# Gate stage of a two-block expert kernel: one-hot rows of the first index made on GpSimd

## Chip, cores and metric

The kernel runs on one core of one Trainium2 chip. The metric is device time in microseconds of one execution, the median over several runs. Lower is better.

## What is computed

Two transformer blocks run one after the other on 256 tokens of width 1024, all in float32. Each block ends in a layer of product-key experts. The part of it that matters here, cut from the reference:

```python
qh = (t @ w_q).reshape(T, PEER_HEADS, 2, PEER_KEY_DIM // 2)
s = jnp.einsum('thpd,hpnd->thpn', qh, sub_keys)           # 128 keys per half
s_top, i_top = lax.top_k(s, PEER_TOPK)                    # 16 of each half
best, pos = lax.top_k(cand.reshape(T, PEER_HEADS, 256), PEER_TOPK)
idx = ...                                                 # i1 * 128 + i2
g = jax.nn.softmax(best, axis=-1)
act = jax.nn.gelu(jnp.einsum('thkd,td->thk', u_tab[idx], t))
out = jnp.einsum('thk,thkd->td', g * act, v_tab[idx])
```

Each token chooses 8 heads x 16 = 128 experts of 128 x 128 = 16384, each named by a first index, a second index and a gate.

## The kernel before, in words

The kernel gathers no expert rows. For each block it streams both whole tables (128 units of 512 KB each) and multiplies densely. In the **u loop** TensorE makes, for every unit, the products of 128 experts with all 256 tokens, and ScalarE writes their GELU into `arena` (`acts`, 128 experts x 128 units x 256 tokens). In the **v loop** the same array, multiplied by the gates, is contracted with the v table. Both loops split float32 into a rounded part and a rest: ScalarE casts (L1377, L1599), VectorE subtracts (L1380, L1606), TensorE does three passes (L1308 to L1310).

Between the two loops stands the **gate stage**, once per block. It turns the chosen pairs of indices into a dense table of gates and multiplies `acts` by it. It takes the 256 tokens in 32 groups of 8 (`NG = 32`). For a group:

- VectorE copies the group's five columns per token out of `sel` into `stage[slot]` (L1535, 128x40): first index, second index, gate, minus the second index, minus the gate; the partition is the choice. It raises the semaphore `staged`.
- VectorE makes `hot1` in one instruction (L1537, 128x1024): for each of the 8 tokens, row k of a 128x128 tile is 1 at the first index of choice k and 0 elsewhere.
- `hot2`, the same with the second index and the gate in place of 1, is shared. VectorE makes tokens 4 to 7 with one two-operation instruction each (L1540, 128x128, equality with the second index, then times the gate). ScalarE makes tokens 0 to 3 in two instructions each (L1549: absolute distance to the index; L1553: Relu of gate minus gate times distance). `ACT_HOT = 4` is this number.
- TensorE (`pe_gates`, L1565) multiplies hot1 by hot2 for each of the 8 tokens into two of the eight PSUM banks.
- VectorE (`dve_multiply`, L1574, 128x1024) multiplies the group's 8 token columns of `acts` by those two banks, in place.

Order and waits. hot1, hot2 and `stage` have four slots, and so has PSUM (two banks each). VectorE's order is written out by hand: hots of group 0, hots of 1, then for each g: hots of g + 2, multiply of g (`HOT_AHEAD = 2`). Before it stages a group, VectorE waits until TensorE has used the slot's former group (`e_ready`). TensorE waits for both makers of the hots (`hots_dve`, `hots_act`) and for the multiply four groups back (`gated`). The multiply waits for `e_ready` of its own group. When all 32 are multiplied, ScalarE, VectorE and TensorE enter the v loop together. The stream's ring (four units) is filled by the SP queue, which stands still during this stage since nothing consumes. GpSimd runs one instruction of the program, a memset of a 128x128 tile of ones at its very start (L1753), and nothing after it.

All hots read `iota`, a 128x128 constant loaded at the start (`common_loaded`).

Of the kernel before, what the change touches and what calls it, by code (L numbers as in the profile page):

```python
# [26 lines left out]
ALU = mybir.AluOpType  # L27
# [3 lines left out]
P = 128  # L31
# [20 lines left out]
HLRING = 4  # L52
CRING = 4
GRING = 4
ACT_HOT = 4
NPROJ = 3
B_STAT = (3, 7)
B_SCORE = (4, 5)
# [191 lines left out]
def build(nc, stream, xT, ctxT, metaT, vectors, common, consts1, consts2, keys1, keys2, w_a2, out):  # L250
# [45 lines left out]
    def c_(name):  # L296
        a, n = con_at[name]
        return con[:, a:a + n]

    ident, blk64, iota, ones = c_("ident"), c_("blk64"), c_("iota"), onesbuf[:, :]  # L300
# [23 lines left out]
    def S(name):  # L324
        if name not in sems:
            sems[name] = nc.alloc_semaphore(name)
        return sems[name]
# [114 lines left out]
    hot1 = gbuf[:, 0:GRING * 8 * P].rearrange("p (r t i) -> p r t i", r=GRING, t=8)  # L442
    hot2 = gbuf[:, GRING * 8 * P:2 * GRING * 8 * P].rearrange("p (r t i) -> p r t i", r=GRING, t=8)
    H = Space(gbuf, 10240)
    H.take(8192)
    stage = [H.take(KINDS, 8) for _ in range(GRING)]
    hot_dist = [H.take(ACT_HOT, P) for _ in range(2)]

# [450 lines left out]
    class Rope:  # L899
# [14 lines left out]
        def pe(self, eng):  # L914
            for r in self.ready:
                wait(eng, *r)
            for i, (src, _) in enumerate(self.items):
                m = self.r0 + i
                wait(eng, "rope_read", m - 1)
                eng.matmul(ps[:, B_STAT[m % 2], 0:self.n], self.rot, src, start=True, stop=True).then_inc(S("rope_swapped"), 1)  # L920
# [482 lines left out]
    def topk_part(eng, i, s, half):  # L1403
# [16 lines left out]
        if n == 3:  # L1420
            for x, _, rest in halves_of:
                eng.max(topbuf[:, x, 8:16], rest)
# [102 lines left out]
    NG = T // 8  # L1525
    HOT_AHEAD = 2

    def base(b):

        return (b - 1) * (NG + GRING)  # L1530

    def dve_hots(dve, b, g, slot_):

        dve.wait_ge(S("e_ready"), g + (base(b) + 1))
        dve.tensor_copy(stage[slot_], sel[:, :, ds(g * 8, 8)]).then_inc(S("staged"), 1)  # L1535
        dve.wait_ge(S("staged"), g + ((b - 1) * NG + 1))
        dve.tensor_tensor(hot1[:, slot_, :, :], stage[slot_][:, 0, :].rearrange("p (t o) -> p t o", o=1).broadcast_to([P, 8, P]),  # L1537
                          iota.rearrange("p (o i) -> p o i", o=1).broadcast_to([P, 8, P]), ALU.is_equal)
        for t in range(ACT_HOT, 8):
            ins = dve.tensor_scalar(hot2[:, slot_, t, :], iota, stage[slot_][:, 1, t:t + 1],  # L1540
                                    stage[slot_][:, 2, t:t + 1], ALU.is_equal, ALU.mult)
        ins.then_inc(S("hots_dve"), 1)

    def act_hots(act, b, g, slot_):

        act.wait_ge(S("staged"), g + ((b - 1) * NG + 1))
        st, dist = stage[slot_], hot_dist[slot_ % 2]
        for t in range(ACT_HOT):
            ins = act.activation(dist[:, t, :], iota, ACT.Abs, bias=st[:, 3, t:t + 1])  # L1549
        ins.then_inc(S("hot_dist_ready"), 1)  # L1550
        act.wait_ge(S("hot_dist_ready"), g + ((b - 1) * NG + 1))
        for t in range(ACT_HOT):
            ins = act.activation(hot2[:, slot_, t, :], dist[:, t, :], ACT.Relu, bias=st[:, 2, t:t + 1], scale=st[:, 4, t:t + 1])  # L1553
        ins.then_inc(S("hots_act"), 1)

    def e_banks(slot_):
        return ps[:, 2 * slot_:2 * slot_ + 2, :].rearrange("p s n -> p (s n)")

    def pe_gates(pe, b, g, slot_):

        pe.wait_ge(S("hots_dve"), g + ((b - 1) * NG + 1))
        pe.wait_ge(S("hots_act"), g + ((b - 1) * NG + 1))
        pe.wait_ge(S("gated"), g + (base(b) + 1))
        for t in range(8):
            mm = pe.matmul(e_banks(slot_)[:, t * P:(t + 1) * P], hot1[:, slot_, t, :], hot2[:, slot_, t, :],  # L1565
                           start=True, stop=True)
        mm.then_inc(S("e_ready"), 1)
# [8 lines left out]
    def ds(a, n):  # L1576
        return bass.ds(a, n) if not isinstance(a, int) else slice(a, a + n)
# [44 lines left out]
    def peer_pe(pe, b):  # L1622

        pe.wait_ge(S("peer_in"), b)
        pe.drain().then_inc(S("split_used"), HLRING)
        pe.wait_ge(S("hsplit_ready"), b)
        u_loop("pe", pe, b, 0, NQ // UB, table="wq")
        peer_pe_scores(pe, b)
        pe.wait_ge(S("peer_s_copied"), 8 * b)
        with pe.Fori(0, TOPK_IT) as i:  # L1630
            for s in range(TOPK_UB):
                u_unit("pe", pe, b, i, s, TOPK_UB)
        for n in range(MID_UNITS):
            u_unit("pe", pe, b, 0, MID_AT + n)
            pe_gate_part(pe, b, n)
        u_loop("pe", pe, b, MID_END // UB, N_IT)

        pe.wait_ge(S("u_bank_free"), banks_freed(b + 1, "wq"))
        pe.wait_ge(S("sel_taken"), b)
        pe.drain().then_inc(S("e_ready"), GRING)  # L1640
        pe.drain().then_inc(S("gated"), GRING)
        with pe.Fori(0, NG // GRING) as i:
            for n in range(GRING):
                pe_gates(pe, b, i * GRING + n, n)
        pe.wait_ge(S("gated"), b * (NG + GRING))
        v_loop("pe", pe, b)
# [29 lines left out]
    def peer_dve(dve, b):  # L1676
# [11 lines left out]
        for g in range(HOT_AHEAD):  # L1688
            dve_hots(dve, b, g, g)
        with dve.Fori(0, NG // GRING - 1) as i:  # L1690
            for n in range(GRING):
                dve_hots(dve, b, i * GRING + (n + HOT_AHEAD), (n + HOT_AHEAD) % GRING)
                dve_multiply(dve, b, i * GRING + n, n)
        for g in range(NG - GRING, NG):
            if g + HOT_AHEAD < NG:
                dve_hots(dve, b, g + HOT_AHEAD, (g + HOT_AHEAD) % GRING)
            dve_multiply(dve, b, g, g % GRING)
# [13 lines left out]
    with nc.Block() as block:  # L1711
        @block.sync
        def _(sp):

            peer_units = {u: n for n, u in enumerate(m for key in ("wq1", "u1", "v1", "wq2", "u2", "v2") for m in units[key])}

            def load(u):
                sp.dma_start(slot(u), stream[u, :, :]).then_inc(S(arrival(u)[0]), 16)

            u = 0  # L1720
            while u < n_units:
                old = u - RING
                if u in peer_units and old in peer_units:

                    end = u
                    while end < n_units and end in peer_units:
                        end += 1
                    rounds = (end - u) // RING
                    n0 = peer_units[old]
                    with sp.Fori(0, rounds) as i:  # L1730
                        for s in range(RING):
                            sp.wait_ge(S("split_lo"), i * 2 * RING + 2 * (n0 + s + 1))
                            sp.dma_start(slot(u + s), stream[bass.ds(i * RING + (u + s), 1), :, :]
                                         .rearrange("a p n -> (a p) n")).then_inc(S(ring_full[(u + s) % RING]), 16)
                    u += rounds * RING
                    while u < end:
                        sp.wait_ge(S("split_lo"), 2 * (peer_units[u - RING] + 1))
                        load(u)
                        u += 1
                    continue  # L1740
                if old in peer_units:
                    sp.wait_ge(S("split_lo"), 2 * (peer_units[old] + 1))
                elif old >= 0:
                    sp.wait_ge(S("tile_done"), last_tile[old] + 1)
                load(u)
                u += 1
            sp.wait_ge(S("peer_out"), 2 * KD)
            sp.dma_start(out, resid[:, :, :]).then_inc(S("out_stored"), 16)
            sp.wait_ge(S("out_stored"), 16)

        @block.gpsimd
        def _(pool):
            pool.memset(ones, 1.0).then_inc(S("ones_ready"), 1)  # L1753

        @block.scalar
        def _(act):
# [167 lines left out]
```

## Time and profile before

| | before |
|---|---|
| runs | 2661.96, 2658.42, 2659.87 us; median 2659.87 |
| profiled execution, span from first to last instruction | 2658.5 us |
| TensorE busy | 2445.7 us (92%) |
| VectorE busy | 1683.0 us (63%) |
| ScalarE busy | 1293.7 us (49%) |
| GpSimd busy | 0.4 us |
| mean granted TensorE clock | 0.973 of 2.4 GHz |

The profiled execution has no time of its own beside its span. The span lies 1.4 us below the median of the runs and 0.1 us above the fastest of them. How to read the profile: a group of instructions is one line of the code on one engine with its shapes, its count, its total busy time and the mean duration of one instruction. Instructions on one engine overlap a little, so the step from start to start is shorter than a duration. Idle time before an instruction is put down to the instruction that ended it.

### The profile page before, as it was taken

Reading aid. Unit: us, or ns where it says so; the run is one execution under the profiler, and the core shown is the slowest. Engines: PE = TensorE matmul, PEld = TensorE weight load, DVE = VectorE, ACT = ScalarE, POOL = GpSimd, SP = SyncE. Lnnn points to the kernel's source line nnn. Section 1 sums busy time; section 2 is a strip of 40 time slices with the busy share of each in tenths; the row PEclk is TensorE's granted clock in tenths of the full one; section 3 lists DMA queues with packets and bytes.
Section 4 is the critical chain, followed back from the end, with each engine's and each line's share of the span. In section 5 each row is a group of like instructions: output and inputs, shape, how many; then the busy total and the mean of one; then the engine's idle time right before and its main releaser. Section 6 shows DMA issues by size and latency. Waiting matters only on the chain.

```text
span 2658.5 us, 51578 instructions
## 1 busy us (share of the span) xinstructions
PE 2445.7 (92%) x17556; PEld 2270.0 (85%) x17556; DVE 1683.0 (63%) x3490; ACT 1293.7 (49%) x2816; POOL 0.4 (0%) x5
## 2 busy tenths in 40 slices
PE   7999979999985799999799999889999985899998
PEld 2767879999985799999677777789999985899998
DVE  2565247888769766665225674238888769766665
ACT  1456145555568655554123422055555568555554
POOL 0000000000000000000000000000000000000000
PEclk9989989999999999999899899999999999999999
DMA  6345444555530355555232212445555530355554
GB/s 229 136 168 189 150 143 163 183 183 181 184 119 0 103 182 182 183 183 178 98 127 88 80 56 80 135 142 183 181 181 182 183 103 0 121 182 183 183 184 143
DMA packets 108502, 388.94 MB, mean 146 GB/s; under 512 B 12784, under 2 KB 15088, under 8 KB 107776
## 3 DMA queue, kind: packets, MB, share of 16 engines
q1 hardware_dynamic: 104256, 380.16, 42.5%
q10 hardware_dynamic: 4160, 7.61, 0.9%
q8 instruction: 58, 0.95, 0.1%
q14 instruction: 28, 0.23, 0.0%
HBM read 386.67 MB, written 1.05 MB: 146 GB/s over the span
## 4 chain that ended last, share of the span: by engine, by line
PE 84%; DVE 9%; issue 3%; ACT 2%; DVEq 0%; ACTq 0%; DMA 0%; PEld 0%; PEldq 0%
PE ps L1308 20%; PE ps L1310 20%; PE ps L1309 20%; PE ps L707 19%; DVE arena L1574 2%; DVE gbuf L1540 2%; PE ps L789 2%; PE ps L1000 1%; PE ps L978 1%; PE ps L1565 1%; PE ps L1340 1%; DVE gbuf L801 0%; PE ps L992 0%; PE ps L1236 0%; ACT arena L772 0%
## 5 line engine op out<-in xcount | busy, mean ns | idle before, releaser
L1308 PE MATMUL ps<-hsplit,hl 128*128 128x256 f32 x2304 | 655.9, 285 | 31.7 <-DVE hl L1380 31.7
L1309 PE MATMUL ps<-hsplit,hl 128*128 128x256 f32 x2304 | 655.0, 284 | 0.0
L1310 PE MATMUL ps<-hsplit,hl 128*128 128x256 f32 x2304 | 654.9, 284 | 0.0
L1308 PE MATMUL ps<-csplit,hl 128*128 128x256 f32 x2048 | 581.1, 284 | 6.2 <-DVE hl L1606 6.2
L1309 PE MATMUL ps<-csplit,hl 128*128 128x256 f32 x2048 | 581.0, 284 | 0.0
L1310 PE MATMUL ps<-csplit,hl 128*128 128x256 f32 x2048 | 581.0, 284 | 0.0
L1377 ACT CAST hl<-ring 128x512 fp32r<-128x512 f32 x576 | 355.6, 620 | 387.2 <-PE ps L1310 386.8
L1380 DVE TENSOR_TENSOR hl<-ring,hl 128x512 fp32r<-128x512 f32 x576 | 397.6, 692 | 221.2 <-ACT hl L1377 187.4
L1308 PEld LDWEIGHTS ps<-hsplit,hl 128*128 128x128 f32 x2304 | 445.7, 193 | 32.8 <-ACT hl L1377 32.8
L707 PE MATMUL ps<-arena,ring 128*128 128x256 f32 (+2 forms) x1896 | 447.6, 395 | 15.5 <-issue 10.8
L1309 PEld LDWEIGHTS ps<-hsplit,hl 128*128 128x128 f32 x2304 | 445.7, 193 | 0.0
L1310 PEld LDWEIGHTS ps<-hsplit,hl 128*128 128x128 f32 x2304 | 445.4, 193 | 0.0
L707 PEld LDWEIGHTS ps<-arena,ring 128*128 128x128 f32 x1896 | 369.2, 197 | 78.8 <-issue 25.7
L1606 DVE TENSOR_TENSOR hl<-ring,hl 128x512 fp32r<-128x512 f32 x512 | 354.3, 693 | 92.8 <-ACT hl L1599 91.6
L1308 PEld LDWEIGHTS ps<-csplit,hl 128*128 128x128 f32 x2048 | 394.6, 193 | 6.5 <-issue 6.5
L1310 PEld LDWEIGHTS ps<-csplit,hl 128*128 128x128 f32 x2048 | 394.6, 193 | 0.0
L1309 PEld LDWEIGHTS ps<-csplit,hl 128*128 128x128 f32 x2048 | 394.6, 193 | 0.0
L1599 ACT CAST hl<-ring 128x512 fp32r<-128x512 f32 x512 | 315.8, 617 | 109.9 <-PE ps L1310 109.9
L1603 DVE TENSOR_TENSOR csplit<-arena,csplit 128x256 fp32r<-128x256 f32 x256 | 109.0, 426 | 183.0 <-ACT csplit L1598 183.0
L1598 ACT CAST csplit<-arena 128x256 fp32r (+1 forms) x256 | 104.2, 407 | 235.5 <-PE ps L1310 228.5
L1565 PE MATMUL ps<-gbuf 128*128 128x128 f32 x1024 | 133.0, 285 | 92.7 <-ACT gbuf L1553 49.1
L1565 PEld LDWEIGHTS ps<-gbuf 128*128 128x128 f32 x1024 | 122.2, 196 | 103.4 <-issue 52.2
(196 smaller groups left out, 2019.7 us busy)
## 6 DMA issues: line engine op xcount, KB each, us to landing
ring<-stream SPq DMA_DIRECT2D x723, 512.0 KB, 3.3
arena<-keys ACTq DMA_DIRECT2D x2, 1024.0 KB, 4.9
gbuf<-consts ACTq DMA_DIRECT2D x1, 1120.0 KB, 5.1
arena<-xT ACTq DMA_DIRECT2D x1, 1024.0 KB, 10.4
arena<-ctxT ACTq DMA_DIRECT2D x1, 1024.0 KB, 12.7
resid<-xT ACTq DMA_DIRECT2D x1, 1024.0 KB, 8.9
out<-resid SPq DMA_DIRECT2D x1, 1024.0 KB, 3.9
gbuf<-consts ACTq DMA_DIRECT2D x1, 832.0 KB, 6.3
```

Source lines behind the costliest of these rows:

```text
L707: mm = pe.matmul(ps[0:t.rows, t.bank, 0:t.cols], lhs, rhs, start=(t.start and i == 0), stop=(t.stop and i == last))
L789: mm = eng.matmul(ps[:, bank, 0:self.cols], self.lhs, self.squares[:, k, 0:self.cols], start=(i == 0), stop=(i == len(group) - 1))
L1308: pe.matmul(out_ap, w[0], m[0], start=start, stop=False)
L1309: pe.matmul(out_ap, w[1], m[0], start=False, stop=False)
L1310: return pe.matmul(out_ap, w[0], m[1], start=False, stop=stop)
L1377: eng.copy(hl[:, hslot, 0, :], raw).then_inc(S("split_hi"), 1)
L1380: eng.tensor_tensor(hl[:, hslot, 1, :], raw, hl[:, hslot, 0, :].bitcast(F32), ALU.subtract)\
L1565: mm = pe.matmul(e_banks(slot_)[:, t * P:(t + 1) * P], hot1[:, slot_, t, :], hot2[:, slot_, t, :], start=True, stop=True)
L1598: eng.copy(csplit[:, cslot, 0, :], acts[:, c]).then_inc(S("csplit_hi"), 1)
L1599: eng.copy(hl[:, hslot, 0, :], slot(unit)[:, part]).then_inc(S("split_hi"), 1)
L1603: eng.tensor_tensor(csplit[:, cslot, 1, :], acts[:, c], csplit[:, cslot, 0, :].bitcast(F32), ALU.subtract)
L1606: eng.tensor_tensor(hl[:, hslot, 1, :], slot(unit)[:, part], hl[:, hslot, 0, :].bitcast(F32), ALU.subtract).then_inc(S("split_lo"), 1)
```

## The change

GpSimd gets a loop over both blocks and all 32 groups. For each group it waits for `staged` and makes hot1 in eight instructions of 128x128, one per token, and token 3 of hot2. ScalarE makes tokens 0 to 2. VectorE no longer makes hot1, and still makes tokens 4 to 7 of hot2. TensorE waits for a third semaphore, `hots_pool`.

```diff
-ACT_HOT = 4
+ACT_HOT = 3
+POOL_HOT = 1
 ...
         dve.tensor_copy(stage[slot_], sel[:, :, ds(g * 8, 8)]).then_inc(S("staged"), 1)
         dve.wait_ge(S("staged"), g + ((b - 1) * NG + 1))
-        dve.tensor_tensor(hot1[:, slot_, :, :], stage[slot_][:, 0, :].rearrange("p (t o) -> p t o", o=1).broadcast_to([P, 8, P]),
-                          iota.rearrange("p (o i) -> p o i", o=1).broadcast_to([P, 8, P]), ALU.is_equal)
-        for t in range(ACT_HOT, 8):
+        for t in range(ACT_HOT + POOL_HOT, 8):
             ins = dve.tensor_scalar(hot2[:, slot_, t, :], iota, stage[slot_][:, 1, t:t + 1],
                                     stage[slot_][:, 2, t:t + 1], ALU.is_equal, ALU.mult)
         ins.then_inc(S("hots_dve"), 1)
+
+    def pool_hots(pool, b, g, slot_):
+
+        pool.wait_ge(S("staged"), g + ((b - 1) * NG + 1))
+        st = stage[slot_]
+        for t in range(8):
+            pool.tensor_scalar(hot1[:, slot_, t, :], iota, st[:, 0, t:t + 1], None, ALU.is_equal)
+        for t in range(ACT_HOT, ACT_HOT + POOL_HOT):
+            ins = pool.tensor_scalar(hot2[:, slot_, t, :], iota, st[:, 1, t:t + 1], st[:, 2, t:t + 1],
+                                     ALU.is_equal, ALU.mult)
+        ins.then_inc(S("hots_pool"), 1)
 ...
         pe.wait_ge(S("hots_act"), g + ((b - 1) * NG + 1))
+        pe.wait_ge(S("hots_pool"), g + ((b - 1) * NG + 1))
 ...
             pool.memset(ones, 1.0).then_inc(S("ones_ready"), 1)
+            pool.wait_ge(S("common_loaded"), 16)
+            for b in (1, 2):
+                for g in range(NG):
+                    pool_hots(pool, b, g, g % GRING)
```

## Rows read from the trace of the kernel before

**Rows 1.** Timeline of the first gate stage, its start: start us, us, engine, line, work

```profile
776.43 0.19 DVE L1535 COPY gbuf<-s_area 128x40 f32<-128x40 f32 x1 [4.94 <-PEq L1640]
776.66 1.22 DVE L1537 TENSOR_TENSOR gbuf<-gbuf,con 128x1024 f32<-128x1024 f32 x1
779.72 5.44 PE L1565 MATMUL ps<-gbuf 128*128 128x128 f32 x32 [3.85 <-ACT gbuf L1553]
783.60 1.21 DVE L1574 TENSOR_TENSOR arena<-arena,ps 128x1024 f32 x1
```

**Rows 2.** Timeline of the first gate stage, its end and the v loop's first instruction

```profile
885.68 2.34 DVE L1574 TENSOR_TENSOR arena<-arena,ps 128x1024 f32<-128x1024 f32 x2
886.58 2.02 PE L1565 MATMUL ps<-gbuf 128*128 128x128 f32 x16 [1.51 <-DVE gbuf L1540]
888.64 1.22 DVE L1574 TENSOR_TENSOR arena<-arena,ps 128x1024 f32<-128x1024 f32 x1 [0.61 <-PE ps L1565]
889.89 0.40 ACT L1598 CAST csplit<-arena 128x256 fp32r<-128x256 f32 x1 [3.41 <-DVE arena L1574]
```

**Rows 3.** Timeline of the second gate stage: its first instruction and the one behind it

```profile
2165.66 0.19 DVE L1535 COPY gbuf<-s_area 128x40 f32<-128x40 f32 x1 [4.94 <-PEq L1640]
...
2279.29 0.40 ACT L1598 CAST csplit<-arena 128x256 fp32r<-128x256 f32 x1 [3.57 <-DVE arena L1574]
```

**Rows 4.** Timeline in the middle of the first gate stage: one whole group

```profile
841.05 0.19 DVE L1535 COPY gbuf<-s_area 128x40 f32 x1
841.27 1.23 DVE L1537 TENSOR_TENSOR gbuf<-gbuf,con 128x1024 f32<-128x1024 f32 x1
841.27 1.28 ACT L1549 ACTIVATE gbuf<-con,gbuf 128x128 f32<-128x128 f32 x4 [0.56 <-DVE gbuf L1535]
842.42 1.11 DVE L1540 TENSOR_SCALAR gbuf<-con,gbuf 128x128 f32<-128x128 f32 x4
842.59 1.65 ACT L1553 ACTIVATE gbuf<-gbuf 128x128 f32<-128x128 f32 x4
843.44 1.21 DVE L1574 TENSOR_TENSOR arena<-arena,ps 128x1024 f32 x1
844.33 2.02 PE L1565 MATMUL ps<-gbuf 128*128 128x128 f32 x16 [1.50 <-DVE gbuf L1540]
844.57 0.18 DVE L1535 COPY gbuf<-s_area 128x40 f32 x1
```

**Rows 5.** Groups by line and shape, 782 to 884 us: busy us, mean ns | idle before

```profile
L1553 ACT ACTIVATE gbuf<-gbuf 128x128 f32<-128x128 f32 x118 | 48.6, 482 | 1.0
L1549 ACT ACTIVATE gbuf<-con,gbuf 128x128 f32<-128x128 f32 x118 | 37.8, 390 | 15.4 <-DVE gbuf L1535 15.4
L1540 DVE TENSOR_SCALAR gbuf<-con,gbuf 128x128 f32<-128x128 f32 x116 | 32.2, 341 | 0.0
```

**Rows 6.** Busy time in 5 us stretches: PE, PEld, DVE, ACT, POOL, PEclk, DMA, GB/s

```profile
775.00:780.00 5.00, 1.15 (x10) 0.98 (x9) 3.50 (x8) 3.69 (x11) 0.00 (x0) 1.00 0.00 2
780.00:785.00 5.00, 5.00 (x32) 4.96 (x30) 4.93 (x14) 4.93 (x15) 0.00 (x0) 0.66 0.00 0
840.00:845.00 5.00, 2.69 (x22) 2.56 (x23) 4.93 (x11) 3.85 (x11) 0.00 (x0) 1.00 0.00 0
```

**Rows 7.** Timeline of GpSimd, the whole span

```profile
0.24 0.10 POOL L1918 MEMSET const-float32-0.0<- 128x1 f32 x1 [0.24 <-issue]
0.74 0.20 POOL L1753 MEMSET onesbuf<- 128x128 f32 x1 [0.29 <-POOLq L1918]
```

**Rows 8.** Groups by line and shape on VectorE, the whole span

```profile
L801 DVE RECIPROCAL gbuf<-gbuf 128x256 f32<-128x256 f32 x20 | 35.1, 1753 | 0.7
L1185 DVE TENSOR_TENSOR arena<-gbuf 128x128 f32<-128x128 f32 x56 | 12.5, 285 | 0.3
...
L1506 DVE TENSOR_SCALAR s_area<-ps 128x256 f32<-128x256 f32 x2 | 0.8, 419 | 0.0
L1469 DVE TENSOR_SCALAR gbuf<-gbuf 128x256 f32<-128x256 f32 x2 | 0.6, 285 | 0.0
```

## The prediction

> **What bounds the kernel now.** I read the page first: TensorE carries the span, and only the two gate stages lie between its long loops. So I read each gate stage by its edges, then one group in its middle, then its groups of instructions. In the timeline the first stage begins with the copy at 776.43 us and ends with the last multiply, 888.64 + 1.22 = 889.86 us; the first cast of the v loop starts 0.03 us later [rows 1, 2]. The second stage runs from 2165.66 to just before 2279.29 us [rows 3]. That is 113.4 and 113.6 us, 227 us together, 8.5% of the span. All that follows waits for it, so a microsecond here is a microsecond of the kernel.
>
> Within a stage one group takes 844.57 - 841.05 = 3.52 us, and VectorE is never idle in it [rows 4]: in the stretch from 840 to 845 us it is busy 4.93 of 5 us, TensorE 2.69, ScalarE 3.85 [rows 6]. By start-to-start steps, VectorE's group is the copy with its own wait 0.22 us, hot1 1.15, four rows of hot2 1.02, the multiply 1.13. ScalarE has slack: 1.32 us to the start of the Relus and 1.65 for them, 2.97 in all, and it sits idle 0.56 us for the copy. TensorE needs 2.02 us and waits 1.50 [rows 4]. From the last group's matmuls to the end there are 2.06 us of TensorE and 1.22 of multiply [rows 2]. VectorE is the bound, and no DMA moves: the DMA share is 0.00 [rows 6].
>
> **The change part by part.**
>
> *hot1 leaves VectorE.* One instruction per group, 1.15 us by the step. VectorE is left with 0.22 + 1.02 + 1.13 = 2.37 us per group. That is the floor on this engine.
>
> *One row of hot2 leaves ScalarE.* Two instructions per group. An Abs steps by (1.28 - 0.39) / 3 = 0.30 us and a Relu by (1.65 - 0.48) / 3 = 0.39 us [rows 4, 5], so ScalarE goes from 2.97 to about 2.3 us. It was not the bound. It matters only where the others fall near 2.4 us, where four rows would have held the group at 2.97.
>
> *TensorE's third wait.* It is one more instruction in TensorE's queue ahead of matmuls that wait 1.50 us anyway; I cost it at nothing. What is queued behind it are the group's matmuls and then, in VectorE's queue, the multiply and the staging of the third group on. The stage has room for that. From the end of GpSimd's group g to its group g + 3 being staged are about 2.06 + 1.22 + 0.2 = 3.5 us, against two groups of GpSimd's work in between.
>
> *GpSimd's nine instructions.* This is the new term, and everything turns on it. They stand in one queue with nothing else in it; the wait for `common_loaded` was over hundreds of microseconds before. If one takes t, GpSimd needs 9t per group, from the first staging at 776.66 us on [rows 1]. If it sets the pace, the stage ends at 776.66 + 32 x 9t + 3.4, the last being TensorE's 2.06, the multiply's 1.22 and about 0.1 of hand-over. Setting that equal to 889.86 gives 9t = 3.43 us, t = 0.381 us: **the break-even**. Each 0.01 us on t moves the kernel by 64 x 9 x 0.01 = 5.8 us.
>
> The trace of before has no GpSimd instruction that reads. The nearest from below is the memset of 128x128, 0.20 us; the memset of 128x1 takes 0.10, so a fixed part of 0.10 and another 0.10 for 128 columns that are only written [rows 7]. The upper end, far off, is VectorE's slow reciprocal, 1.753 us for 256 columns, so some 0.9 for 128, the price of an operation that takes many steps per element [rows 8]. Ends: 9t = 1.8 and 8.1 us. Between them I build from the nearest row. To the memset's 0.20 I add 0.10 for 128 columns read, 0.10 for 128 comparisons (one more turn of the same loop each), and 0.06 for fetching the per-partition operand: VectorE's instruction with such operands takes 0.341 us where one of the same size without takes 0.285 [rows 5, 8]. That is t = 0.46 us. I take it for the two-operation row too. ScalarE's instructions of this shape, 0.39 and 0.48 us, lie on both sides of it [rows 5]. So 9t = 4.14 us against 3.52 today. The stage ends at 776.66 + 132.5 + 3.4 = 912.5 us, 22.7 us later; two stages make **+45 us**. VectorE falls idle 4.14 - 2.37 = 1.8 us per group, and TensorE waits for GpSimd.
>
> The Trainium skill, "GPSIMD Engine Reference", section 3.1, gives a best case of 1.8 cycles per element at 1.2 GHz for a tight loop, with further fixed costs (section 7: about 102 cycles for a read command). An estimate from that page is 0.19 + 0.09 = 0.28 us for one instruction, by which the change would gain; the trace of before shows no such instruction.
>
> *TensorE's clock.* It is granted 1.00 in the middle of the stage, with TensorE idle 1.50 us out of 3.52, and 0.66 in the stretch behind the 3.85 us of idleness at its start [rows 4, 6]. At 4.14 us per group the idle stretch is 2.1 us. If the grant fell to 1.2 GHz, the matmuls would take 4.04 us, still under 4.14, so only the last group would show it, 2 us per stage. I cost it at nothing.
>
> The sum is made on the profiled execution, 2658.5 + 45.4 = 2703.9 us. The median of the runs lies 1.4 us above that span, so **2705 us**, 1.7% slower. A measurement of this kernel can tell about 0.2%, 5.3 us, from no change.
>
> **The rivals.**
>
> *GpSimd is fast enough (the other side).* Place: the same nine instructions. Below t = 0.381 us the change gains, until at t = 0.26 us VectorE's 2.37 us take over. At t = 0.30 us GpSimd still sets the pace: 776.66 + 86.4 + 3.4 = 866.5, 23.4 us earlier per stage, 2613 us. With VectorE the bound, 32 x 2.37 = 75.8 us and some 2.7 for the first products give a stage of 78.5, 35 us less, 2590 us. For it speak the memset's 0.10 us for 128 columns, and the slack on ScalarE and TensorE, which can both follow to 2.4. Against it, a memset reads nothing and compares nothing. I give the paced gain 0.24 and the VectorE floor 0.14.
>
> *GpSimd and VectorE take turns.* Both now work at the same time on the same memory. If a VectorE instruction that reads and writes only that memory with one input shuts GpSimd out, and the reverse, the copy (0.19) and the four rows of hot2 (1.11) add to GpSimd's time: 4.14 + 1.30 = 5.44 us per group. The stage ends at 776.66 + 174.1 + 3.4 = 954.2, 64.3 us later, and the kernel takes 2789 us. The durations of L1540 on VectorE would then scatter upward from 0.341. For it: with its source in SBUF a 128x256 instruction takes 0.285 us, with its source in PSUM 0.419, so the former moves the columns at about twice the rate, as if by a second path [rows 8]. Against it: no trace of before has the two engines at work together. Chance 0.15. With this in force, break-even is at t of about 0.24 us, so it would also eat a fast GpSimd's gain. The rule is one of the Trainium skill, "SBUF — State Buffer", section "Who interferes with whom": a VectorE instruction in a 2-port mode and a GpSimd instruction hold the shared port pair in turn, each for its whole length. The two durations agree with its 2-port mode; no run here shows the lock.
>
> *GpSimd is slower still.* At t above 0.6 us, the lines above give more than 2786 us, up to 2959 at 0.9. Chance 0.05.
>
> *Nothing visible.* 9t near 3.43 us, within 0.08 either way: 0.06.
>
> **How the numbers follow.** The forecast's case, GpSimd alone setting the pace with t between 0.39 and 0.6 us, has 0.36. Slower: 0.36 + 0.15 + 0.05 = 0.56. Faster: 0.24 + 0.14 = 0.38. Same: 0.06. The likeliest case's own range is 2665 to 2786 us. The range that should hold the time 8 times in 10 must take in both signs: it goes down to the VectorE floor, 2588, and up to the taking of turns, 2792. Outside lie the very slow GpSimd and about half of the taking of turns, where t is above 0.46 too, and a small rest below.
>
> **What would show it.** In the profile after, GpSimd has 576 new instructions of 128x128, and their step from start to start is t. Right: the period of L1535 is 9t, over 3.52 us, TensorE's idle time before L1565 is put down to GpSimd, VectorE waits before L1574, ScalarE waits longer before L1549, and the u and v loops are unchanged. The prediction is wrong if a step is under 0.38 us, or if VectorE's L1540 grows and its group no longer fits in 2.37 us, or if time appears outside the two stages.

## The result and the profile after

The changed kernel takes 2790.51 us (median), against 2659.55 us for the kernel before in the runs beside it: ratio 1.0491, interval 1.0478 to 1.0504. It is 131 us slower where the prediction had 45 slower. The profiled execution spans 2789.3 us.

The page of the kernel after: busy time by engine, GpSimd and the clock in 40 slices, and the chain that ended last.

```profile
PE 2511.3 (90%) x17556; PEld 2333.3 (84%) x17556; DVE 1625.0 (58%) x3426; ACT 1249.7 (45%) x2688; POOL 350.5 (13%) x581
POOL 0000000000089600000000000000000099400000
PEclk9989999999977799999899899999999977799999
PE 79%; POOL 13%; DVE 4%; ACT 2%; issue 1%; DMA 0%; ACTq 0%; PEld 0%; DVEq 0%; POOLq 0%; PEldq 0%
L1548 POOL TENSOR_SCALAR gbuf<-con,gbuf 128x128 f32<-128x128 f32 x512 | 300.5, 603 | 2052.7 <-DVE gbuf L1536 2052.7
```

GpSimd is busy only in the two gate stages, and there without a gap. It holds 13% of the chain; before, the larger part of the chain in these stages was VectorE's hot2 rows and multiplies (L1540 and L1574, 2% of the whole span each). The lines have moved: L1548 is the hot1 rows on GpSimd, L1550 its hot2 row, L1539 VectorE's rows (L1540 before), L1576 the products (L1565), L1585 the multiply (L1574).

Timeline of the kernel after, one stretch of the first stage (start, length, work; in brackets the idle time and what ended it), answering to [rows 4]:

```profile
844.29 0.18 DVE L1536 COPY gbuf<-s_area 128x40 f32 x1
844.51 1.24 DVE L1539 TENSOR_SCALAR gbuf<-con,gbuf 128x128 f32<-128x128 f32 x4
845.41 0.84 POOL L1550 TENSOR_SCALAR gbuf<-con,gbuf 128x128 f32<-128x128 f32 x1
846.24 4.64 POOL L1548 TENSOR_SCALAR gbuf<-con,gbuf 128x128 f32<-128x128 f32 x8
846.55 3.60 PE L1576 MATMUL ps<-gbuf 128*128 128x128 f32 x16 [3.54 <-POOL gbuf L1550]
850.30 1.22 DVE L1585 TENSOR_TENSOR arena<-arena,ps 128x1024 f32 x1 [4.55 <-PE ps L1576]
850.87 0.79 POOL L1550 TENSOR_SCALAR gbuf<-con,gbuf 128x128 f32<-128x128 f32 x1
851.63 4.85 POOL L1548 TENSOR_SCALAR gbuf<-con,gbuf 128x128 f32<-128x128 f32 x8
```

Everyone waits for GpSimd: TensorE 3.54 us, and VectorE for TensorE 4.55 us. GpSimd's own steps from start to start are 4.63 / 8 = 0.58 us for a row of hot1 and 0.76 and 0.83 for the row of hot2, some 0.78. Two starts 28 groups apart, and the end of the stage, from the same execution:

```profile
791.50 4.64 POOL L1548 TENSOR_SCALAR gbuf<-con,gbuf 128x128 f32<-128x128 f32 x8
...
944.83 4.63 POOL L1548 TENSOR_SCALAR gbuf<-con,gbuf 128x128 f32<-128x128 f32 x8
...
952.56 1.22 DVE L1585 TENSOR_TENSOR arena<-arena,ps 128x1024 f32<-128x1024 f32 x1 [2.41 <-PE ps L1576]
953.81 0.40 ACT L1609 CAST csplit<-arena 128x256 fp32r<-128x256 f32 x1 [13.19 <-DVE arena L1585]
```

A group takes (944.83 - 791.50) / 28 = 5.48 us, where it took 3.52. The stage starts at 774.54 and ends at 953.8: 179.3 us against 113.4 [rows 1, 2]. That is 65.9 us more. The second stage takes 180.4 us against 113.6, 66.8 us more. Together they make some 133 us, where the two profiled spans differ by 130.8: all of the loss lies in the two stages.

### The profile page after: what moved, and what is told of

Read it like the earlier page. It is cut to its first block, busy times and chain, and to the rows that moved or that the text cites. A ratio compares the mean times of both kernels' runs of the same rounds, so it can differ in the third digit from the quotient of the medians.

```text
span 2789.3 us, 51997 instructions
## 1 busy us (share of the span) xinstructions
PE 2511.3 (90%) x17556; PEld 2333.3 (84%) x17556; DVE 1625.0 (58%) x3426; ACT 1249.7 (45%) x2688; POOL 350.5 (13%) x581
## 4 chain that ended last, share of the span: by engine, by line
PE 79%; POOL 13%; DVE 4%; ACT 2%; issue 1%; DMA 0%; ACTq 0%; PEld 0%; DVEq 0%; POOLq 0%; PEldq 0%
PE ps L1309 19%; PE ps L1310 19%; PE ps L1311 19%; PE ps L708 18%; POOL gbuf L1548 11%; POOL gbuf L1550 2%; PE ps L790 1%; PE ps L1001 1%; PE ps L979 1%; PE ps L1341 1%; DVE gbuf L802 0%; DMA ring<-stream 0%; PE ps L993 0%; PE ps L1237 0%; ACT arena L773 0%
## 5 line engine op out<-in xcount | busy, mean ns | idle before, releaser
L1548 POOL TENSOR_SCALAR gbuf<-con,gbuf 128x128 f32<-128x128 f32 x512 | 300.5, 603 | 2052.7 <-DVE gbuf L1536 2052.7
L1576 PE MATMUL ps<-gbuf 128*128 128x128 f32 x1024 | 200.8, 376 | 157.4 <-POOL gbuf L1550 145.5
L1576 PEld LDWEIGHTS ps<-gbuf 128*128 128x128 f32 x1024 | 186.0, 281 | 172.1 <-issue 91.3
```

Of the source, the lines that this page charges most:

```text
L1548: pool.tensor_scalar(hot1[:, slot_, t, :], iota, st[:, 0, t:t + 1], None, ALU.is_equal)
```

## The experiments

Two theories stood after the result. Theory A: GpSimd's own price is higher than the 0.46 us that I built up. Theory B: the price was about right, and the rest comes from GpSimd and VectorE taking turns, the second rival, whose 2789 us is almost exactly the measured time. The number alone can't tell them apart.

**e1, hot1 alone on GpSimd.** One execution.

```diff
-ACT_HOT = 3
-POOL_HOT = 1
+ACT_HOT = 4
+POOL_HOT = 0
```

> GpSimd makes hot1 alone (8 instructions per group), ScalarE again makes four rows of hot2. Theory A, GpSimd's own price sets the pace (0.585 us per hot1 row, 0.78 for the hot2 row, by the steps in the trace after): a group takes 8 x 0.585 = 4.7 us in place of 5.5, and each stage ends 25 us earlier than after the change, some 2740 us in all. Theory B, the time comes mostly from GpSimd and VectorE taking turns: VectorE's instructions are the same, so a group still carries their 1.3 us, and a group takes 8 x 0.46 + 1.3 = 5.0 us.

It took 2743.5 us. The first stage ran from 779.3 to 932.9 us, 153.6 us, and GpSimd's groups start 4.67 us apart. That is theory A's number, where theory B had 5.0.

**e2, no rows by VectorE.** One execution.

```diff
+        dve.wait_ge(S("e_ready"), base(b) + GRING)
+        dve.memset(hot2[:, :, 4:8, :], 0.0).then_inc(S("hots_dve"), 1)
...
-        for t in range(ACT_HOT + POOL_HOT, 8):
-            ins = dve.tensor_scalar(...)
-        ins.then_inc(S("hots_dve"), 1)
...
-        pe.wait_ge(S("hots_dve"), g + ((b - 1) * NG + 1))
+        pe.wait_ge(S("hots_dve"), b)
```

> VectorE makes no rows of hot2 in the loop (rows 4 to 7 are zeros, so the gates of those tokens are left out): only the copy and the multiply stand beside GpSimd. Theory A (own price): GpSimd's steps stay at about 0.58 us, a group takes 5.4 us, the time falls by under 8 us against the changed kernel. Theory B (turns with VectorE's single-input instructions): GpSimd's steps fall to about 0.46 us and a group to 4.3 us, some 2715 us in all.

It took 2793.2 us. GpSimd's timeline in it:

```profile
940.45 4.69 POOL L1544 TENSOR_SCALAR gbuf<-con,gbuf 128x128 f32<-128x128 f32 x8
945.08 0.84 POOL L1546 TENSOR_SCALAR gbuf<-con,gbuf 128x128 f32<-128x128 f32 x1
945.85 4.69 POOL L1544 TENSOR_SCALAR gbuf<-con,gbuf 128x128 f32<-128x128 f32 x8
```

With VectorE's four rows gone, a group still takes 945.85 - 940.45 = 5.40 us. The turns were worth 5.48 - 5.40 = 0.08 us per group to GpSimd, not 1.30: for this change theory B falls. The stages are a little shorter, 177.9 us against 179.3 and 178.3 against 180.4, 3.5 us together. The whole time did not drop, since the rest of this execution was 5.6 us longer (it entered the first stage at 778.2 us and not at 774.5). The four runs of the changed kernel differ by more than that, from 2788 to 2796 us.

**e3, a price list.** The kernel before with nine GpSimd instructions per group beside it, writing to free memory. They stand here in the order of the lines below. TensorE still waits for the semaphore that the last of the nine raises, so the list sets the pace of the stage. One execution.

```diff
+        pool.memset(z[0], 0.0)
+        pool.tensor_copy(z[1], iota)
+        pool.tensor_scalar(z[2], iota, 3.0, None, ALU.is_equal)
+        pool.tensor_scalar(z[3], iota, st[:, 0, 0:1], None, ALU.is_equal)
+        pool.tensor_scalar(z[4][:, 0:64], iota[:, 0:64], st[:, 0, 0:1], None, ALU.is_equal)
+        pool.tensor_scalar(s_area[:, 1024:1280], con[:, 0:256], st[:, 0, 0:1], None, ALU.is_equal)
+        pool.tensor_scalar(z[5], iota, st[:, 0, 0:1], None, ALU.mult)
+        pool.tensor_tensor(z[6], iota, ident, ALU.subtract)
+        pool.tensor_scalar(z[7], iota, st[:, 1, 0:1], st[:, 2, 0:1], ALU.is_equal, ALU.mult)
```

> The kernel before, with nine GpSimd instructions per group beside it whose results are not used: memset, copy, compare with a constant, compare with a per-partition operand at 128, 64 and 256 columns, multiply, subtract of two tensors, compare and multiply. The prediction's working: 0.20 us for the memset, 0.30 for the copy, 0.40 for the comparison with a constant, 0.46 with a per-partition operand. Rival: the fixed part is what was missed, so 64 columns cost nearly as much as 128 (0.45 or more against 0.58), and 256 columns 0.8. Other rival: the work per column was missed, so 64 columns cost about 0.3 and 256 about 1.1 us.

It took 2793.7 us, with a new group every 5.54 us. Timeline of GpSimd over one group; VectorE is idle beside it from the memset to the subtraction:

```profile
853.51 0.20 POOL L1553 MEMSET s_area<- 128x128 f32 x1
853.66 0.29 POOL L1554 COPY s_area<-con 128x128 f32<-128x128 f32 x1
853.92 0.54 POOL L1555 TENSOR_SCALAR s_area<-con 128x128 f32<-128x128 f32 x1
854.44 0.60 POOL L1556 TENSOR_SCALAR s_area<-con,gbuf 128x128 f32<-128x128 f32 x1
855.02 0.44 POOL L1557 TENSOR_SCALAR s_area<-con,gbuf 128x64 f32<-128x64 f32 x1
855.43 0.92 POOL L1558 TENSOR_SCALAR s_area<-con,gbuf 128x256 f32<-128x256 f32 x1
856.32 0.61 POOL L1559 TENSOR_SCALAR s_area<-con,gbuf 128x128 f32<-128x128 f32 x1
856.90 0.45 POOL L1560 TENSOR_TENSOR s_area<-con 128x128 f32<-128x128 f32 x1
857.34 0.80 POOL L1561 TENSOR_SCALAR s_area<-con,gbuf 128x128 f32<-128x128 f32 x1
```

From start to start: memset 0.15 us, copy 0.26, comparison with a constant 0.52, with a per-partition operand 0.58, the same at 64 columns 0.41 and at 256 columns 0.89, multiplication 0.58, subtraction of two tensors 0.44; compare and multiply lasts 0.80. The step from copy to arithmetic with one operand, 0.26 us, is as large as the copy. It isn't the comparison, since a multiplication costs the same. From the three widths a column costs 2.4 to 2.7 ns, which leaves a fixed part of 0.58 - 128 x 0.0025 = 0.26 us. The measured 0.41 and 0.89 us lie between the two rivals of the expectation, nearer to the one with the fixed part.

The same view a group earlier, with VectorE's hot1 (L1538, two inputs in SBUF) beside GpSimd:

```profile
847.26 1.25 DVE L1538 TENSOR_TENSOR gbuf<-gbuf,con 128x1024 f32<-128x1024 f32 x1
847.41 1.51 POOL L1555 TENSOR_SCALAR s_area<-con 128x128 f32<-128x128 f32 x1
...
850.87 1.36 DVE L1538 TENSOR_TENSOR gbuf<-gbuf,con 128x1024 f32<-128x1024 f32 x1
851.36 1.18 POOL L1560 TENSOR_TENSOR s_area<-con 128x128 f32<-128x128 f32 x1
```

An instruction of 0.54 us takes 1.51, one of 0.45 takes 1.18; both end 0.3 to 0.4 us behind the end of L1538. So turns do exist, against the two-input instruction that the change had taken off VectorE. Another group shows both sides, a memset and a copy that start while L1538 runs:

```profile
863.64 1.22 DVE L1538 TENSOR_TENSOR gbuf<-gbuf,con 128x1024 f32<-128x1024 f32 x1
863.85 0.20 POOL L1553 MEMSET s_area<- 128x128 f32 x1
864.00 1.01 POOL L1554 COPY s_area<-con 128x128 f32<-128x128 f32 x1
```

The copy takes 1.01 us instead of 0.29. The memset (L1553) lasts between 204 and 205 ns in all its 64 places, and 28 of them lie inside L1538. The Trainium skill, "SBUF — State Buffer", section "Who interferes with whom", says that a VectorE instruction with two SBUF inputs contends with a GpSimd instruction that reads SBUF, and not with one that only writes it. This trace agrees: the reads are held up, the memset is not.

**e4, three rows of hot2 on GpSimd, hot1 back on VectorE.** Rows of hot2: ScalarE 3, GpSimd 3, VectorE 2.

```diff
-POOL_HOT = 1
+POOL_HOT = 3
+        dve.tensor_tensor(hot1[:, slot_, :, :], ...)
-        for t in range(8):
-            pool.tensor_scalar(hot1[:, slot_, t, :], ...)
```

> hot1 is back on VectorE; GpSimd makes three rows of hot2 (tokens 3 to 5), ScalarE three, VectorE two. Theory A (own price): GpSimd 3 x 0.78 = 2.35 us per group, VectorE 0.22 + 1.15 + 0.51 + 1.13 = 3.0 us, ScalarE 2.3: VectorE sets the pace at 3.0 to 3.1 us against 3.52 before, 26 to 33 us faster than before, about 2630 us. Theory B (turns): the 1.15 us of hot1 and the others on VectorE add to GpSimd's 2.35, so 3.5 us or more, no gain over before.

2640.96 us, ratio to before 0.9922 (0.9905 to 0.9938): faster than before. Two steps in its timeline, and the group of GpSimd's rows from 790 to 880 us:

```profile
841.25 1.25 DVE L1538 TENSOR_TENSOR gbuf<-gbuf,con 128x1024 f32<-128x1024 f32 x1
844.29 1.25 DVE L1538 TENSOR_TENSOR gbuf<-gbuf,con 128x1024 f32<-128x1024 f32 x1
```
```profile
L1550 POOL TENSOR_SCALAR gbuf<-con,gbuf 128x128 f32<-128x128 f32 x87 | 88.3, 1028 | 0.9 <-DVE gbuf L1536 0.9
```

The group takes 3.04 us as theory A had it, with VectorE full. But GpSimd is full too: a row lasts 1.03 us on average instead of 0.79. Of the 31 us only 20 came, since the stage is 103.4 us, 6.4 more than 32 groups of 3.03, while before it was 0.8 more than 32 groups of 3.52 [rows 1, 2, 4]: the ends of the stage give back a part.

**e5, the same without hot1.** hot1 is zero, set once per stage by VectorE.

```diff
-        dve.tensor_tensor(hot1[:, slot_, :, :], ...)
+        dve.wait_ge(S("e_ready"), base(b) + GRING)
+        dve.memset(hot1, 0.0)
```

> The last kernel (three rows of the second index on GpSimd), but VectorE makes no rows of the first index: they are zeros, so all gates are left out. Theory A (VectorE's two-input instruction L1538 shuts GpSimd's out for its length): GpSimd's mean falls from 1.04 to 0.80 us, a group takes 2.35 to 2.4 us, some 2600 us. Theory B (GpSimd is slowed by anything else, or its clock of work follows the pace of the stage): its mean stays over 0.95 us, the group 2.9 us or more.

2606.3 us, one execution. GpSimd's rows from 790 to 860 us:

```profile
L1548 POOL TENSOR_SCALAR gbuf<-con,gbuf 128x128 f32<-128x128 f32 x87 | 70.1, 821 | 0.9 <-DVE gbuf L1536 0.9
```

The mean falls from 1.028 to 0.821 us, and the group to 2.4 (87 rows in 70 us). Taking L1538 away, with one memset per stage in its place, gives GpSimd its own price back. Theory A of this run is shown.

**e6, half of hot1 on GpSimd.** Tokens 0 to 3 of hot1 and token 3 of hot2.

```diff
-        for t in range(8):
+        for t in range(4):
             pool.tensor_scalar(hot1[:, slot_, t, :], ...)
+        dve.tensor_tensor(hot1[:, slot_, 4:8, :], ...)
```

> GpSimd makes tokens 0 to 3 of hot1 and token 3 of hot2, VectorE tokens 4 to 7 of both, with one two-input instruction of 128x512 for hot1. GpSimd's own price is 4 x 0.58 + 0.78 = 3.1 us, VectorE's 0.22 + 0.62 + 1.02 + 1.13 = 3.0 us. Without turns the group takes 3.1 us, 27 us faster than before in all (2633). With turns against the two-input instruction (0.6 us per group) it takes 3.7 to 3.8 us, 12 to 18 us slower than before (about 2675).

2654.9 us, ratio 0.9983 (0.9973 to 0.9993). Both sizes were off. Timeline:

```profile
843.20 0.88 DVE L1538 TENSOR_TENSOR gbuf<-gbuf,con 128x512 f32<-128x512 f32 x1
845.88 2.53 POOL L1550 TENSOR_SCALAR gbuf<-con,gbuf 128x128 f32<-128x128 f32 x4
846.49 0.88 DVE L1538 TENSOR_TENSOR gbuf<-gbuf,con 128x512 f32<-128x512 f32 x1
```

The group is 3.29 us. The two share the loss: VectorE's 128x512 takes 0.88 us, where the shortest of this line takes 0.69, and GpSimd's four rows 2.53 instead of 4.64 / 2 = 2.32. In nearly every group one GpSimd row is already running when L1538 starts and is not longer for it; the next starts inside L1538 and takes 0.80 instead of 0.60. VectorE, which came second to the first of them, lost 0.19 us and not the 0.57 that this row still had to run.

**e7, rows of hot2 four, three, one.** ScalarE 4, GpSimd 3, VectorE 1; against e4:

```diff
-ACT_HOT = 3
+ACT_HOT = 4
```

> Three rows of hot2 on GpSimd, four on ScalarE, one on VectorE, hot1 on VectorE. Theory A (turns with the two-input instruction): GpSimd needs 2.35 plus about 0.7 of waiting, 3.05 us, as in the kernel with three, three and two, so the time is the same within 5 us, about 2641. Rival: GpSimd's waiting there was only VectorE's pace seen from the other side, and the group falls to ScalarE's 2.97 or VectorE's 2.78 us, 4 to 12 us faster, 2629 to 2637 us.

2651.8 us, ratio 0.9969 (0.9955 to 0.9984): slower than e4, which neither theory had. GpSimd's row from 790 to 860 us:

```profile
L1550 POOL TENSOR_SCALAR gbuf<-con,gbuf 128x128 f32<-128x128 f32 x65 | 71.1, 1109 | 0.0
```

Three rows at 1.109 us are 3.3 us: GpSimd has no idle time and is shut out for longer, 0.9 us per group against 0.7. One row of each kernel that starts inside L1538, e4 first (L1538 from 841.25 to 842.50), then e7 (from 841.57 to 842.80):

```profile
841.76 1.50 POOL L1550 TENSOR_SCALAR gbuf<-con,gbuf 128x128 f32<-128x128 f32 x1
```
```profile
841.63 1.92 POOL L1550 TENSOR_SCALAR gbuf<-con,gbuf 128x128 f32<-128x128 f32 x1
```

In e4 it starts 0.51 us behind the start of L1538, in e7 0.06. Both end some 0.75 us behind the end of L1538, almost their whole own length of 0.79. So the loss is what is left of L1538 when the row starts, and in e7 the rows start earlier in it (0.24 us in the median). Why they do was not settled.

**e8, hot1 in single-input instructions.** From e4; VectorE makes hot1 in eight instructions of 128x128.

```diff
-        dve.tensor_tensor(hot1[:, slot_, :, :], ...)
+        for t in range(8):
+            dve.tensor_scalar(hot1[:, slot_, t, :], iota, stage[slot_][:, 0, t:t + 1], None, ALU.is_equal)
```

> As the three, three and two kernel, but VectorE makes hot1 in eight single-input instructions of 128x128 in place of the two-input one. If only a two-input instruction shuts GpSimd out, GpSimd's mean is 0.80 us and VectorE sets the pace at 0.22 + 8 x 0.255 + 0.51 + 1.13 = 3.9 us or a little more, about 2685 us. If single-input ones do it too, GpSimd's mean stays near 1.0 us, and VectorE's instructions rise from 0.33 to 0.5 us or more, the group to over 4.5 us, 2725 us or more.

2664.2 us, one execution. Timeline:

```profile
843.77 1.81 DVE L1539 TENSOR_SCALAR gbuf<-con,gbuf 128x128 f32<-128x128 f32 x8
843.84 2.76 POOL L1550 TENSOR_SCALAR gbuf<-con,gbuf 128x128 f32<-128x128 f32 x3 [0.83 <-DVE gbuf L1536]
```

VectorE sets the pace at 3.60 us. Its eight instructions step by 0.216 us, less than the 0.255 I had put in. GpSimd's three rows take 2.76 us instead of 2.35, beside ten single-input instructions. So these cost GpSimd something, 0.4 us here, but far from their whole length. Each rival of the expectation had a part: GpSimd's mean of 0.93 us lies between the two, and VectorE's own rows did not grow to 0.5.

**e9, rows four, two, two.** ScalarE 4, GpSimd 2, VectorE 2, hot1 on VectorE; against e4:

```diff
-ACT_HOT = 3
-POOL_HOT = 3
+ACT_HOT = 4
+POOL_HOT = 2
```

> Four rows of hot2 on ScalarE, two on GpSimd, two on VectorE, hot1 on VectorE. VectorE: 0.21 + 1.18 + 0.51 + 1.13 = 3.03 us per group, ScalarE 2.97, GpSimd 2 x 0.78 + 0.65 of being shut out = 2.2. If GpSimd's pace was what the three, three and two kernel stood at, this one, with GpSimd idle 0.8 us per group, does as well or a little better, since no row comes late at the ends of the stage: 2630 to 2642 us. If three engines near 3 us hinder each other (ScalarE's and VectorE's groups no longer overlap freely, as in the four, three and one kernel at 3.2 us), 2645 to 2655 us.

**2630.58 us, ratio 0.9896 (0.9879 to 0.9912)**: it beats both kernels. Timeline:

```profile
842.00 1.22 DVE L1538 TENSOR_TENSOR gbuf<-gbuf,con 128x1024 f32<-128x1024 f32 x1
842.06 2.69 POOL L1550 TENSOR_SCALAR gbuf<-con,gbuf 128x128 f32<-128x128 f32 x2 [0.32 <-DVE gbuf L1536]
845.00 1.22 DVE L1538 TENSOR_TENSOR gbuf<-gbuf,con 128x1024 f32<-128x1024 f32 x1
```

The group is 3.00 us. GpSimd's first row starts 0.06 us behind the start of L1538 and is shut out for 2.69 - 1.56 = 1.1 us, almost the whole of it; GpSimd still has 0.32 us to spare. The stage takes 100.1 us against e4's 103.4.

## Why the prediction was right and wrong

**Bound and path: right.** The two stages were where the time went, and 776.66 + 32 x 9t + 3.4 held as a form: with 5.48 us it gives a stage of 0.2 + 175.4 + 3.4 = 179.0 us, measured 179.3. No run stands at the break-even of 3.43 us. The nearest, e6 at 3.29 us, has a stage of 110.5 us (108.9 by the form), 2.9 shorter than before, and is 0.17% faster.

**The price t: wrong, and it is the step that failed.** "That is t = 0.46 us. I take it for the two-operation row too." Measured by steps it is 0.58 and 0.78 us. Taken apart by e3: the 0.10 for reading was right (memset 0.15, copy 0.26), the 0.06 for the per-partition operand too (0.52 to 0.58). The 0.20 for the memset was a duration; its step is 0.15. The 0.10 for "128 comparisons (one more turn of the same loop each)" is 0.26, and the second operation with its operand, counted as nothing, is another 0.2. It was not the turns of the loop that were dear: the prediction's own parts give 0.16 us fixed and 0.30 for 128 columns, and with them 0.31, 0.46 and 0.76 us at 64, 128 and 256 columns, where e3 has 0.41, 0.58 and 0.89. Of the 0.12 us missing at 128 columns some 0.10 is fixed per instruction. In the sum: 8 x 0.12 + 0.32 = 1.28 us per group missing, plus 0.06 of disturbance by VectorE, against 4.14 taken. Times 64 that is 86 us, the whole gap between 45 and 131. The memset, though on the right engine, was the wrong neighbour for an instruction that computes.

**The range: luck.** 2588 to 2792 us holds the measured 2790.5, but its upper end had been set for the taking of turns. The case that came, GpSimd alone with t above 0.6 us, was one that the prediction put outside its range, with a chance of 0.05.

**The estimate of 0.28 us** was further off. The Trainium skill, "GPSIMD Engine Reference", section 3.1, has 1.8 cycles per element at 1.2 GHz in the best case, an estimate of 1.5 ns a column. e3's steps show 2.4 to 2.7 ns, and 0.26 us of fixed cost. The measurement decides.

**ScalarE and VectorE: right.** VectorE's four rows lasted 1.24 us in place of 1.11, its copy and multiply as before, and both engines then waited.

**TensorE's clock: right in kind.** The grant fell where the idle stretches grew: over the two stages it was 0.72 and 0.70, where in the middle of the stage before it was 1.00 [rows 6]. In the last group of the second stage it was 0.50, which is 1.2 GHz, and the products took 3.78 us instead of 2.05 there (2.02 in the first stage). View by stretch (both stages, and that last group), and timeline, of the kernel after:

```profile
774.00:954.00 180.00, 99.21 (x512) 92.29 (x512) 82.29 (x192) 72.26 (x194) 175.32 (x288) 0.72 0.00 0
2229.00:2409.00 180.00, 101.62 (x512) 93.70 (x512) 82.75 (x191) 71.55 (x192) 174.72 (x288) 0.70 0.00 0
2403.00:2408.00 5.00, 3.78 (x16) 3.49 (x16) 0.23 (x1) 0.00 (x0) 0.72 (x1) 0.50 0.00 0
```
```profile
2403.96 3.78 PE L1576 MATMUL ps<-gbuf 128*128 128x128 f32 x16 [2.46 <-POOL gbuf L1550]
```

It cost 1.7 us once, within the 2 us per stage that the prediction named; elsewhere the slower products stay under GpSimd's pace.

**Taking turns: right number, wrong cause.** It gave 2789 us with t = 0.46 and 1.30 us of turns. e2 measured 0.08 us of turns. VectorE's L1539 went from 0.341 to 0.378 us in the median (up to 0.75), so VectorE loses about 0.04 us per instruction, which it had to spare. Neither size fits the rule that the prediction set beside this rival, by which each holds off the other for its whole length. Its argument for the rival was weak as well: 0.285 us against 0.419 is a ratio of 1.5, and "about twice the rate" only if some 0.15 us of each is fixed, which no row shows. The mechanism is real but belongs to the instruction with two inputs, which the change removed; I had looked for it only among the single-input ones. The third rival, t above 0.6 us, is where the kernel came out (5.48 / 9 = 0.61).

## What to carry to other kernels

Moving work to an idle engine pays only if all that this engine then does in a group, waits on the other engine included, fits under the new pace. Eight 128x128 comparisons cost GpSimd 4.64 us and saved VectorE 1.15: GpSimd became the bound, above the 3.52 us of before. Two two-operation rows cost it 2.69 us with all that it was shut out, for 0.51 us saved, a poorer rate, and made the kernel 1% faster, since 2.69 is still under the 3.00 us at which VectorE then went. Measure the other engine's price for this very kind of instruction first, by a list of such instructions beside the kernel; a cheaper kind on the same engine is a poor neighbour. When a rival's number fits the result, still take its cause away before you believe it.

## What was not expected of the hardware

- GpSimd's copy of 128x128 float32 steps by 0.26 us, a comparison or multiplication of it with one value by 0.52 to 0.58, a subtraction of two tensors by 0.44, less than the operation with one tensor and an operand (e3).
- A VectorE instruction with two SBUF inputs holds up a GpSimd instruction that reads and starts while it runs, until it ends (1.1 us of 1.22 in e9, 0.7 in e4). It does not lengthen itself when GpSimd's instruction starts behind it (1.22 us in e9), and loses 0.19 us where one is already running (e6). GpSimd's memset is not touched (e3).
- Ten single-input VectorE instructions held up three GpSimd rows by 0.4 us (e8), and four of them nine rows by 0.08 (the kernel after against e2).
